# Memory keys turned by VectorE through DRAM instead of by TensorE, beside every second pooling output pair and the first FFN

## What is computed

```python
def _mem_attend(h, mk, mv, w_q, w_o):
    q = (h @ w_q).reshape(n, length, MEM_HEADS, MEM_HEAD_DIM)
    sc = jnp.einsum('nlhd,nmhd->nhlm', q, mk).astype(jnp.float32) * (MEM_HEAD_DIM ** -0.5)
    p = jax.nn.softmax(sc, axis=-1).astype(mv.dtype)
    o = jnp.einsum('nhlm,nmhd->nlhd', p, mv).reshape(n, length, MEM_DIM)
    return o @ w_o
# per layer l, samples: mk = cache_mem_k[l] of shape (8, 256, 4, 128), mv = cache_mem_v[l]
```

## Time and profile before

| | us |
|---|---|
| median of 3 runs (2315.04 to 2316.87) | 2315.42 |
| the profiled execution | 2315.27 |
| its span in the profile | 2313.5 |
| TensorE busy | 2298.4 |
| VectorE busy | 1345.1 |
| ScalarE busy | 955.4 |
| GpSimd busy | 163.7 |

### The profile page before, as it was taken

One profiled execution on the slowest core, in us unless ns is written; L12 is line 12 of the kernel. 1 busy time (PEld: TensorE's weight loads), 2 busy tenths in 40 slices (PEclk: granted clock), 3 DMA queues, 4 the chain that ended last, 5 costly groups with the idle time before them and its releaser, 6 DMA issues.

```text
span 2313.5 us, 45948 instructions
## 1 busy us (share of the span) xinstructions
PE 2298.4 (99%) x19092; PEld 2270.4 (98%) x19092; DVE 1345.1 (58%) x1717; ACT 955.4 (41%) x1143; POOL 163.7 (7%) x186
## 2 busy tenths in 40 slices
PE   9999999999999999999999999999999999999999
PEld 8999998999999999999999998899999999999999
DVE  7778557655446565455556776675554455544554
ACT  7434455433333333334444334553333333333333
POOL 0100112000001221000110111110000000000001
PEclk9999999999999999999999999999999999999999
DMA  8665765655557888555565675655555565555553
GB/s 292 196 196 177 242 197 181 194 181 180 177 179 235 246 248 246 180 181 178 176 192 174 201 224 180 217 165 181 181 178 177 181 181 178 178 179 182 178 170 126
DMA packets 385079, 445.88 MB, mean 193 GB/s; under 512 B 14762, under 2 KB 346810, under 8 KB 384446
## 3 DMA queue, kind: packets, MB, share of 16 engines
q1 hardware_dynamic: 371854, 401.72, 55.3%
q0 software_dynamic: 12592, 42.14, 6.4%
q10 hardware_dynamic: 528, 0.52, 0.1%
HBM read 432.50 MB, written 12.74 MB: 192 GB/s over the span
## 4 chain that ended last, share of the span: by engine, by line
PE 98%; DVE 1%; ACT 1%; DMA 0%; issue 0%; DVEq 0%; POOL 0%; ACTq 0%; POOLq 0%
PE acc L819 30%; PE acc L821 30%; PE acc L820 30%; PE acc L896 1%; PE acc L904 1%; PE acc L897 1%; PE ab L1076 0%; DVE wlo L1367 0%; PE acc L1029 0%; PE acc L998 0%; PE acc L1008 0%; PE ab L915 0%; PE ab L998 0%; PE ab L965 0%; DMA att<-in_norm_ffn 0%; PE ab L1112 0%
## 5 line engine op out<-in xcount | busy, mean ns | idle before, releaser
L819 PE MATMUL acc<-xs,whi 128*128 128x264 f32 (+1 forms) x3776 | 1081.3, 286 | 0.0
L821 PE MATMUL acc<-xs,wlo 128*128 128x264 f32 (+1 forms) x3776 | 1073.1, 284 | 0.0
L820 PE MATMUL acc<-xs,whi 128*128 128x264 f32 (+1 forms) x3776 | 1072.1, 284 | 0.0
L482 ACT ACTIVATE whi<-raw 128x1024 fp32r<-128x1024 f32 x744 | 763.1, 1055 | 704.1 <-DMA raw<-in_ffn_w_up 286.8
L1367 DVE TENSOR_TENSOR wlo<-raw,whi 128x1024 fp32r<-128x1024 f32 x744 | 875.9, 1228 | 210.2 <-ACT whi L482 189.5
L821 PEld LDWEIGHTS acc<-xs,wlo 128*128 128x128 f32 x3776 | 713.1, 189 | 0.0
L819 PEld LDWEIGHTS acc<-xs,whi 128*128 128x128 f32 x3776 | 709.2, 188 | 2.0 <-issue 1.1
L820 PEld LDWEIGHTS acc<-xs,whi 128*128 128x128 f32 x3776 | 710.7, 188 | 0.2
L819 PE MATMUL acc<-hA,whi 128*128 128x264 f32 (+1 forms) x1216 | 346.9, 285 | 2.5 <-DVE hA L1656 1.0
L821 PE MATMUL acc<-hA,wlo 128*128 128x264 f32 (+1 forms) x1216 | 345.6, 284 | 0.0
L820 PE MATMUL acc<-hA,whi 128*128 128x264 f32 (+1 forms) x1216 | 344.7, 283 | 0.0
(11 more groups left out here) (296 smaller groups left out, 1155.0 us busy)
## 6 DMA issues: line engine op xcount, KB each, us to landing
raw<-in_ffn_w_gate SPq DMA_DIRECT2D x176, 512.0 KB, 3.5
raw<-in_ffn_w_up SPq DMA_DIRECT2D x176, 512.0 KB, 3.5
raw<-in_ffn_w_down SPq DMA_DIRECT2D x176, 512.0 KB, 3.6
raw<-in_dil_w_q SPq DMA_DIRECT2D x48, 512.0 KB, 3.8
raw<-in_pool_w_in SPq DMA_DIRECT2D x32, 512.0 KB, 3.6
raw<-in_pool_w_out SPq DMA_DIRECT2D x32, 512.0 KB, 3.6
raw<-in_mem_w_v SPq DMA_DIRECT2D x16, 512.0 KB, 7.7
raw<-in_mem_w_k SPq DMA_DIRECT2D x16, 512.0 KB, 5.6
```

The costliest lines, as they stand in the source:

```text
L482: nc.scalar.activation(half_block(whi, n, half), half_block(raw, n, half), ACT.Copy).then_inc(hi_ready, 1)
L819: mm(out, w_hi, hi_, start=first, stop=False)
L820: mm(out, w_hi, lo_, start=False, stop=False)
L821: return mm(out, w_lo, hi_, start=False, stop=last)
```

## The change

TensorE's 128 transposes (16 samples of 8) and ScalarE's 16 copies go, with `kt_ready` and `kt_free`. In their place a layer's keys make four rounds of the pattern above, 1 MB each, with a DRAM tensor `m_turned`: GpSimd loads rows (`turn_memory_rows`), VectorE turns them in blocks (128 x 2048), GpSimd stores them with four DMAs (`store_memory_rows`). The four rounds of layer 0 stand beside `wout`: VectorE's turn comes after the low tiles of items 0, 2, 4 and 6, and GpSimd's stores and loads stand between its sums of squares. The four rounds of layer 1 stand in part 0 of the first FFN, in the last four turns of its loop. The turned keys are then loaded to the same homes with 16 DMAs of 256 KB a layer (`load_memory_keys`): in layer 0 all of them after the last sum of squares and the last store, in layer 1 twelve of them when the dilated attention has ended and four at the start of `mq1`. `sample_scores` waits for these loads (`memory_keys_in`).

```diff
@@ VectorE, wout
                 low_tiles("memq0", 2 * j)
+                if j % 2 == 0:
+                    eng.wait_ge(rows_landed, 8 * j + 16)
+                    v.transpose(memory_rows_turned, memory_rows_in).then_inc(keys_blocked, 1)
@@ VectorE, turn of the FFN's loop
+                        if l == 0 and part == 0 and h is hB:
+                            eng.wait_ge(rows_landed, 16 * i + 16)
+                            v.transpose(memory_rows_turned, memory_rows_in).then_inc(keys_blocked, 1)
                         if l == 0 and part == 1:
-                            eng.wait_ge(rows_landed, 48 * i + 48)
+                            eng.wait_ge(rows_landed, 48 * i + 48 + 128)
@@ GpSimd
+            def turn_memory_rows(l, i):
+                count = 4 * l + i
+                if count:
+                    eng.wait_ge(keys_stored, 64 * count)
+                src = a["cache_mem_k"][l, 2 * i:2 * i + 2]
+                eng.dma_start(memory_rows_in.rearrange("p (b k c) -> p b k c", b=2, k=2),
+                              src.rearrange("b (k p) h d -> p b k (h d)", p=P)).then_inc(rows_landed, 16)
+            def store_memory_rows(l, i):
+                eng.wait_ge(keys_blocked, 4 * l + i + 1)
+                rows = m_turned[(4 * l + i) * BLK:(4 * l + i + 1) * BLK, :].rearrange("(x t) (j s) -> t j x s", t=32, s=32)
+                for j in range(4):
+                    eng.dma_start(rows[:, j], quadrant(memory_rows_turned, j).rearrange("t (x s) -> t x s", s=32)).then_inc(keys_stored, 16)
+            def load_memory_keys(l, i):
+                for b in (2 * i, 2 * i + 1):
+                    for k in range(2):
+                        at = (4 * l + i) * BLK + (2 * (b % 2) + k) * MEMD
+                        eng.dma_start(KTm(b)[:, :, k * P:(k + 1) * P],
+                                      m_turned[at:at + MEMD, :].rearrange("(h d) j -> d h j", d=P)).then_inc(memory_keys_in[i], 16)
...
-            load_first_keys(0)
-            add_squares("memq0")
+            turn_memory_rows(0, 0)
+            for j in range(8):
+                if j:
+                    eng.wait_ge(sq_ready, j + 1)
+                    gp.tensor_tensor(ssq[:, :, :], ssq[:, :, :], sq[:, :, :], ALU.add).then_inc(sq_added, 1)
+                    eng.drain()
+                if j % 2 == 0:
+                    store_memory_rows(0, j // 2)
+                    if j < 6:
+                        turn_memory_rows(0, j // 2 + 1)
+            gp.tensor_tensor(ssq[:, 0, :], ssq[:, 0, :], ssq[:, 1, :], ALU.add).then_inc(sq_added, 1)
+            eng.drain()
+            eng.wait_ge(keys_stored, 64 * 4)
+            load_memory_keys(0, 0)
             load_memory_rows(0)
             add_squares("ffn0")
+            for i in range(4):
+                turn_memory_rows(1, i)
+                store_memory_rows(1, i)
...
@@ GpSimd, end of the dilated attention
-            load_first_keys(1)
+            eng.wait_ge(h_ready, H0["m1"])
+            for i in range(3):
+                load_memory_keys(1, i)
@@ TensorE, samples' scores
-                    eng.wait_ge(kt_free, k0 + TS)
+                    for i in (2 * q, 2 * q + 1):
+                        eng.wait_ge(memory_keys_in[i], 64 * (l + 1))
```

More of the change, by code:

```diff
@@ L84 @@
 for _l in range(2):
-    CACHED += [((f"mk{_l}", i), s) for i, s in enumerate((9, 10, 5, 9))]
     CACHED += [((f"mv{_l}", i), s) for i, s in enumerate((0, 1, 2, 3))]
@@ L173, in sample_values_at @@
             return home, at + b * P
+        memory_rows_in, memory_rows_turned = kx[:, 0:BLK], kx[:, BLK:2 * BLK]
+        m_turned = nc.dram_tensor("m_turned", (2 * 4 * BLK, P), F32, kind="Internal").ap()
         rows_in, rows_turned = kx[:, 0:NG * MEMD], kx[:, NG * MEMD:2 * NG * MEMD]
@@ L254, in trunk @@
         scored = sem("scored")
-        kt_ready, kt_free = sem("kt_ready"), sem("kt_free")
+        memory_keys_in = [sem(f"memory_keys_in{i}") for i in range(4)]
         qz_ready = sem("qz_ready")
@@ L553, in high_items @@
                         upto(N0[f"mo{l}"] + min(i + 3, 5))
[L555 to L559, removed]
             def memory_queries(l):
[L563 to L566, removed]
+                upto(N0[f"mq{l}"] + 2)
                 root(STAT[f"memq{l}"])
-                upto(n + 3)
-                memory_keys_turned(l, 2)
-                memory_keys_turned(l, 3)
+                upto(N0[f"mq{l}"] + 3)
             def mem_attention(l):
@@ L586, in mem_attention @@
                 head_exp(1)
-                memory_keys_turned(l, 4)
                 upto(mo + 1)
-                for b in range(5, TS):
-                    memory_keys_turned(l, b)
                 head_exp(2)
@@ L954, in mem_attention @@
                 n, g = N0[f"mq{l}"], G0[f"mq{l}"]
-                h0, k0 = H0[f"m{l}"], KT0[f"m{l}"]
+                h0 = H0[f"m{l}"]
                 sc, vo = 2 * (g % 2), 2 * ((g + 1) % 2)
@@ L1038, in turn_outputs @@
                     nc.tensor.transpose(ab[:, q, TP:TP + P], Os[:, q, :], ident[:, :]).then_inc(t_ready, 1)
-                pair_item(n, g, 2, xtile, xs_wait(f"memq{l}"), after_first=lambda: statistics(f"memq{l}"),
-                          halves={b: lambda b=b: turn_keys(b) for b in range(4)})
+                pair_item(n, g, 2, xtile, xs_wait(f"memq{l}"), after_first=lambda: statistics(f"memq{l}"))
                 pair_item(n + 2, g + 1, 2, xtile,
-                          halves={0: lambda: (scores(0), scores(1)), 1: lambda: turn_keys(4),
-                                  2: lambda: (turn_probabilities(0), turn_keys(5)), 3: lambda: turn_keys(6)})
+                          halves={0: lambda: (scores(0), scores(1)), 2: lambda: turn_probabilities(0)})
                 weigh(0)
-                turn_keys(7)
                 turn_probabilities(1)
@@ L2057, in taken @@
                 eng.wait_ge(acc_free, g + 1)
+            def turn_memory_rows(l, i):
[16 more added lines that the diff above has]
+                                      m_turned[at:at + MEMD, :].rearrange("(h d) j -> d h j", d=P)).then_inc(memory_keys_in[i], 16)
             def load_memory_rows(l):
                 eng.wait_ge(half_used, 2 * N0[f"mq{l}"])
-                load_cached(eng, (f"mk{l}", 2))
-                eng.wait_ge(kt_ready, KT0[f"m{l}"] + 2)
-                load_cached(eng, (f"mk{l}", 3))
+                for i in (3,) if l else (1, 2, 3):
+                    load_memory_keys(l, i)
                 eng.wait_ge(half_used, 2 * (N0[f"mq{l}"] + 4))
@@ L2067, in load_memory_rows @@
                     load_cached(eng, (f"mv{l}", i))
[L2069 to L2077, removed]
             def quadrant(rows, j, first=0, n=32):
```

10 lines of the change are left out of this document (3 added, 7 removed).

## The result

The changed kernel takes 2327.03 us (median of 6 runs, 2322.49 to 2329.24), the kernel before 2316.85 us beside it (2315.04 to 2316.9). The ratio is 1.0045, 95% interval 1.0035 to 1.0055: slower by 10 us where 8.9 us less was forecast. The profiled execution took 2324.51 us, its span is 2322.6 us, 9.1 us more than before.

What follows compares the result with a forecast made beforehand. TensorE, busy 2298.4 of 2313.5 us, was taken to bound the kernel; 6.8 us in layer 1 plus 2.1 in layer 0 made 8.9 off the 2315.42 median: 2306.5 us (chance 0.50), range 2301 to 2314.

Steps and rivals of the forecast that it cites:

- The worth of the turns: Removing TensorE's eight key turns a layer gives 6.8 us a layer, in layer 0 only 2.1 because loads end last.
- The rounds: Load, VectorE turn and store of 1 MB take 24.0 us against two items' 23.4, falling back 0.6 a round.
- Rival 3: Rounds outlast two items, lag grows in `wout` and FFN: gain zero at 25.7 us, 2329 at 28; chance 0.11.
- the 51 us that a store would take: Skill-based estimate for a round's strided store, making the kernel over 100 us slower; the prediction set it against 10.5 us traced.
- The FFN: Layer 1's four rounds there: the last falls back 1.8 us, inside VectorE's 3 us of idle time; priced at nothing.
- The statistics: Layer 0, behind `wout`: sums ready at 328.6, TensorE wants them at 327.35, a wait of 1.2 us.
- the two turns there: The last two of a layer's eight turns, behind the second `mq` item: worth 1.5 us, between 0.9 and 2.1.
- The key loads and `mo0`: Layer 0: key loads from 335.9, last values at 367.0, `mo0` at 370.6, a gain of 2.1 us, not 6.8.
- Layer 1: Twelve key loads after the dilated attention delay GpSimd's sums at no cost (0 to 1.5 us); gain 6.8, bounds 5 and 8.
- The values: Layer 1: landing takes 12.7 us after the last product against 14.9 until use, so they stay hidden by 2.2 us.

Runs made afterwards that it cites:

- e1: Changed kernel with each drain behind GpSimd's sums of squares replaced by a wait on the sum's own semaphore: 2317.39 us, ratio 1.0008.
- e7: e1 with layer 1's twelve key loads moved behind GpSimd's sums: 2311.89 us.
- e9: e7 with VectorE waiting for GpSimd's seventh sum before its four subtractions in front of the last FFN: 2311.55 us, ratio 0.998.
- e10: e9 plus 16 idle identity transposes in TensorE's dilated-attention wait, and eight layer 0 key loads issued ahead of the wait for the last store: 2307.92 us.
- e4: Changed kernel, all drains kept, with layer 0's last store behind the last sum and layer 1's twelve key loads behind its sums: 2319.99 us.
- e8: e1 plus 16 idle transposing products of the identity in TensorE's wait of the last dilated attention: 2312.86 us.
- e3: Changed kernel with drains replaced at all sums except those for layer 0's `mq0`, which keep theirs: 2319.58 us, ratio 1.0011.

## Why the prediction was wrong

In medians, the way from the measured time to the forecast's 2306.5 is: 2327.0 as it was built, 2317.4 without drains (e1), 2311.9 with layer 1's loads behind the sums (e7), 2311.6 with the sum ahead of VectorE's subtractions (e9), 2307.9 with the idle products and the early key loads (e10).

- **The worth of the turns: the total near, by luck.** The forecast gave the turns 6.8 us a layer and took off 4.7 in layer 0 for late loads: 2.1 + 6.8 = 8.9. The mended change gains 7.6, but in other parts: 5.3 us up to the end of the dilated attention and 1.7 in layer 1 in its profiled execution.
- **The rounds: right.** VectorE's turns in `wout` took 2.30 to 2.31 us (2.4 forecast) and started at 248.97, 272.09, 294.39 and 318.11 (22.3 to 23.7 us apart, where 24 was forecast, and 319.3 for the fourth). From the first store issue to the next load it was 13.03, 12.50 and 12.65 us (the third from 297.01 to 309.66), about the lower end of the 12.8 to 14.0 that came from the earlier trace rows. Rival 3 falls, and with it the 51 us that a store would take by the estimate from the Trainium skill's "VectorE: DVE Perf Modes", The three transpose paths. The Trainium skill states its 19 times there for a large innermost stride at the destination, and these stores write 128 bytes in a row.
- **The FFN: right.** VectorE's four turns there wait for nothing but 0.7 us of issue in all, and the distance to the kernel before stays 2.4 us from `mo0` to about 1380.
- **The statistics: the step that failed.** The prediction says that GpSimd's four store issues "end before it is asked for the sum". They end at 324.91, 0.15 us behind the last squares, so that much is right. But the code has a drain behind every sum, the prediction put it at nothing, and the drain waits for the landing of what was issued: TensorE's wait was 5.15 us instead of 1.2 (0 to 1.8 in the six kernels without these drains), and the lower clock behind it cost 1.28 us in the stretch at 0.50 and 1.32 in the one at 0.67. A gain of 6.8 less 5.15 and 2.6 is a loss of 0.95; `mq0` had begun 0.78 late; that is 1.7 of the 2.4 measured. The other 0.7 lie behind the last product of `mq0`: from there to `mo0` it is 19.3 us, 20.1 before, so the two turns there gave 0.9 us and not 1.5. The row is a wait for VectorE, which the kernel before doesn't have:

```profile
357.59 1.13 PE L967 MATMUL ab<-tmp,mV 128*128 128x256 f32 x4 [1.38 <-DVE tmp L1650]
```

- **The key loads and `mo0`: near once the drains are gone.** Key loads from 333.97 (335.9 forecast). In e1 the last values are used from 366.89 (367.0 forecast), and `mo0` starts at 370.53 (370.6 forecast); in the five kernels without drains in layer 0 and without earlier loads it starts at 370.05 to 373.12. The loads do end last there, but so close a hit is luck: TensorE also waited 3.00 us for keys, and its clock fell to 0.61 behind that (358 to 362), which the forecast did not have and which only took up time that the values would have cost. In the changed kernel TensorE was so late that it waited for no key.
- **Layer 1: the same failed step.** "TensorE has whole blocks in hand there, so I take 0" priced twelve transfers by their issue. The drain held the second sum for 8.18 us. The issue alone costs too: 1.58 us of wait for the statistics in e1, 0.58 with the loads behind the sums (e7, e9). TensorE waited 4.5 us for x (0.9 before), 3.93 for the statistics and 1.76 for the values, and its clock from 1470 to 1478 (0.73 and 0.84) cost 1.5: 3.6 + 3.9 + 1.8 + 1.5 = 10.8 of the 11.0 us missing. The values, taken as hidden by 2.2 us, were not: 1.8 us of wait here, 1.3 to 2.4 in e1, e4, e7, e9 and e10. The forecast counted their 12.7 us from the last product; GpSimd's two issues stand at 1493.16 to 1494.65 and the last product at 1492.58, so the second piece starts more than a microsecond later.
- **TensorE's clock: not in the sum at all.** In the dilated attention 2.0 us are lost in a place that the change doesn't touch. With the idle products the 18 products take 2.25 us again (e8, e10), and the stretch from `mo0` to the first product behind the attention is 1047.1 us, 1048.8 in e1 and 1046.5 before. So the clock is the cause of 1.7 of e1's 2.2 us; the wait itself is 0.35 us longer than before. What decides whether it falls stays open: behind the same gap of 2.36 us it fell in six of the seven kernels of this study that have the change and don't fill the gap, and not in e4.
- **The runs apart from each other.** The changed kernel's profiled run (2324.5) is 2.5 us below its median. The profiled runs of e3, e4 and e8 show the long sum in front of the last FFN (6.04 to 6.10 us), and e9 shows that without it the upper cluster is gone. For the changed kernel itself it is only argued: its runs lie at 2322 to 2325 and 2327 to 2329, and its profiled run, of the lower group, has the short sum (1.59 us). Before, that sum ended ahead of VectorE's subtractions. Why ScalarE's last squares come 0.3 us later in every kernel with the change, so that the two now meet, wasn't found.

## What to carry to other kernels

Ask of every drain on GpSimd what transfers of its own are under way when it runs: in front of a drain a transfer costs the engine its landing, not its issue, and the profile calls this "issue". Order by the producer's own semaphore instead, or put the transfers behind the last drain. And when work is taken out of TensorE, look where its waits grow: a wait of 2.36 us or more was followed here by a lower clock in most kernels, and so cost more than its own length.

## What the hardware showed

- GpSimd's drain waits for its outstanding transfers: 6.38 us (one 1 MB store), 8.18 us (twelve loads of 256 KB), 2.88 us (two spare DMAs of 256 KB), 0.16 us with none.
- After 5.15 us of waiting TensorE had a granted clock of 0.50 in the 4 us stretch in which it went on and 0.67 in the one behind it. After the wait of 2.36 us, ahead of which it had been busy throughout, it had 0.63 in the changed kernel (1404 to 1408) and 0.73 in the one without drains (1400 to 1404), and 1.00 in e4.
- A sum on GpSimd that starts 0.27 us ahead of four VectorE subtractions took 1.54 us in the profiled run of e7 and 6.04 us in that of e8; with 0.33 us ahead it took 1.59 us in the changed kernel and 6.10 in e4.
